# Order of a block's products, masks and stores in the second stage of a two-stage mixer kernel

## The chip, the cores and the metric

The kernel runs on one core of a Trainium2 chip. The metric is the device time of one launch in microseconds (us), the median of several runs. Beside these stands one execution taken with the hardware profiler; all rows below are from that one.

## The reference

One layer `x + RMSNorm_post(Mixer(RMSNorm_pre(x)))` on a prompt of 4096 tokens and on 8 sample streams of 16 tokens, D = 1024. The mixer has a gated linear attention group (4 heads) and an RWKV-7 group (8 heads of 64) that read one input projection and feed one output projection. The change lies in the RWKV-7 group:

```python
def step(s, inp):                      # rwkv7_recurrence, per token
    r_t, w_t, k_t, v_t, kk_t, a_t = inp
    sa = jnp.einsum('bhij,bhj->bhi', s, -kk_t)
    s = (s * w_t[:, :, None, :] + sa[..., None] * (kk_t * a_t)[:, :, None, :]
         + v_t[..., None] * k_t[:, :, None, :])
    y = jnp.einsum('bhij,bhj->bhi', s, r_t)
...
y = ((y - mu) * lax.rsqrt(var + RWKV_GN_EPS)).reshape(B, T, RWKV_WIDTH)   # per head
y = y * rwkv_ln_w + rwkv_ln_b
o_rwkv = (y + bonus) * silu(z_r)
m = jnp.einsum('btc,cd->btd', jnp.concatenate([o_gla, o_rwkv], -1), w_out)
```

## The kernel before

The kernel has two phases. The first (to about 915 us) does the attention group and its projections. The second, `rwkv_phase`, is the one changed. It works on blocks: block 0 holds the 128 sample tokens, blocks 1 to 16 (LAST) hold 256 prompt tokens each. A block has chunks of 64 tokens, four of them for a prompt block. The recurrence is evaluated chunk by chunk in a closed form that needs the inverse of a triangular 64x64 matrix for each chunk and head.

The jobs of one block, and their names in the code:

- `x12, x4, x6, x0, x2, x8, x10`: rounds of the input projection on TensorE, hidden state times weights in split fp16 (three products for each), 128 or 256 output rows each. `x8*4` means four pieces of the round x8; a piece is 8 matmuls of 128x256, and x12 has three pieces, the others six. Each round is then read by ScalarE (`taken`, which writes `praw`) and by VectorE (`mixed`, which writes the operand plane and, as its last instruction, copies the last column to `carry`).
- `lwa0, lwa2` (`rank`, L2140): low-rank products for decay and rate; `kn` and `bs` (`head_sums`, L2179): sums over a head; `clamp`, `rnorm`, `unit`: the key's norm; `k_prime` (L2787, L2788), `beta` (L2801), `a` (`make_a`, L2818), `rkk`, `kappa`, `r`: operands of the recurrence, in `ops`.
- `xs` (`products`, L2158): the block products T^T A of all four chunks, from which the inverse is made. They wait for `beta` and `a` (`op_ok`). `strict:0` and `strict:1` (L2831) mask them into `xb`; `blocks_out` and `blocks_in` on SP's queue store them to DRAM and load them again in another layout; `invert` on GpSimd does 60 dependent steps for the diagonal 32x32 blocks; `inverse_back` stores and reloads the result as `T1` and `TT`, and `td` on VectorE (L2862) transposes `T1`.
- For each chunk: `scores` (L2205), `masked` (VectorE, L2854), `turn` (L2216, L2220), `inner` (L2234), `solve`, `join`, and the state's own chain `meet` (L2289 in the listed rows), `zc` (VectorE, L2886), `unknowns` (L2302), `even`/`odd`, `advance`, `next` (VectorE, L2911, L2913), `keep_y`. `keep_w` (L2870) keeps what `inner` makes; `advance` waits for it.
- For each tile of 128 tokens: `centre`, `variance` (L2357), `deviation`, `normed`, `affine`, `gated`, `high`, `low`: GroupNorm, bonus, gate and the split of m into two fp16 halves; `put_m` stores these.

The order is written out by hand. One table for each engine (`PE_BODY`, `ACT_BODY`, `DVE_BODY`, `SP_BODY`) gives the body for one block b: the projection jobs in it are for block b + 2 (b + 1 with a minus sign), the chunk jobs for block b, and `:4` of `scores`, `inner`, `turn`, `solve`, `join`, `masked`, `keep_w` is the first chunk of block b + 1. `out` marks a point at which work of the output projection is put in near the end of the stage: loads of w_out (`get_ow`), their split into high and low halves (`ow_high` on ScalarE, `ow_low` on VectorE), and jobs that are due when a given number of output units is done. In the last two bodies the pieces of the projection give their place to output units ("room"). Blocks 0 and 1 are prepared by an opening that takes the projection jobs of the same tables in the same order, without chunk jobs.

Four PSUM banks serve all rounds in turn. `ROUND_NO` numbers the rounds in the order of their first piece, bank = number mod 4, and `claim` waits until the round four numbers earlier is read. For x rounds that release is `carry_ok`:

```python
def claim(key):
    m = ROUND_NO[key]
    if m >= NBANK:
        released(ROUND_KEYS[m - NBANK])
    return bank_of(key), m
```

The rounds of a body are numbered in this order: centre:0 (2), x12, bs (2), x4, lw0, la0, lw2, la2, variance:0, x6, x0, kn (2), x2, centre:1 (2), x8, xs0, xs1, variance:1, x10. A counting semaphore `d_full` tells readers that a round is full; its value is the round's number, so rounds must become full in the order of these numbers.

## Time and profile before

| | us |
|---|---|
| median of 3 runs | 2319.01 (2316.41 to 2319.48) |
| profiled execution | 2315.25, its span 2313.5 |
| TensorE busy in the span | 2242.2 (97%) |
| VectorE busy | 1448.1 (63%) |
| ScalarE busy | 1284.4 (56%) |
| GpSimd busy | 578.2 (25%) |
| mean granted clock of TensorE | 0.991 of full speed |

Busy times are sums over a span; times in the rows are us from the span's start. The second phase starts near 925 us; its opening lasts to about 990, the steady bodies to about 1893, block 16's preparation and the last bodies to about 2060, and the rest is the output projection.

### The profile page before, as it was taken

What the parts mean: (1) busy time and instruction counts of PE and PEld (TensorE: products, weight loads), DVE (VectorE), ACT (ScalarE), POOL (GpSimd) and SP (SyncE); (2) the same over time, 40 slices, a digit from 0 to 9 for tenths busy, and PEclk for the clock granted to TensorE, in tenths of its full rate; (3) what the DMA queues carried; (4) which work ended last, traced back from release to release, by engine and by line L of the source; (5) the groups of instructions that cost most, each with busy time, mean ns of one, the idle gap of its engine ahead of it and who ended that gap; (6) DMA issues with size and microseconds to landing.
All of it is one profiled execution on the core that took longest, in us unless ns stands there. A gap on an engine that the chain in (4) does not pass through costs nothing. (4 is left out here: it accounts for less than half of the span.)

```text
span 2313.5 us, 72365 instructions
## 1 busy us (share of the span) xinstructions
PE 2242.2 (97%) x31109; PEld 1704.8 (74%) x31109; DVE 1448.1 (63%) x2699; ACT 1284.4 (56%) x2757; POOL 578.2 (25%) x1070
## 2 busy tenths in 40 slices
PE   7999999999999998889999999999999998899998
PEld 5777777777777776777888888888888886544443
DVE  6444545444455554567777777777777777456675
ACT  8355555555555544645666666666666664343333
POOL 0000000000000000355555555555566565000000
PEclk9999999999999999999999999999999999999999
DMA  6212222222333331222222333232223234666675
GB/s 245 69 56 70 80 79 89 79 79 90 105 108 117 101 101 50 52 59 70 72 72 78 83 87 87 78 81 67 72 82 87 84 88 141 204 213 214 223 237 182
DMA packets 217278, 244.62 MB, mean 106 GB/s; under 512 B 110080, under 2 KB 159552, under 8 KB 212608
## 3 DMA queue, kind: packets, MB, share of 16 engines
q1 hardware_dynamic: 211056, 217.44, 30.8%
q10 hardware_dynamic: 5904, 22.55, 2.7%
q8 instruction: 247, 4.05, 0.7%
q14 instruction: 71, 0.58, 0.1%
HBM read 141.83 MB, written 98.10 MB: 104 GB/s over the span
## 5 line engine op out<-in xcount | busy, mean ns | idle before, releaser
L2111 PE MATMUL first<-h,w_hi 128*128 128x256 f16 (+1 forms) x2496 | 419.1, 272 | 0.0
L2070 POOL TENSOR_TENSOR r_inv_tmp<-r_inv 64x30 f32<-64x30 f32 (+14 forms) x480 | 265.8, 554 | 412.8 <-DMA r_inv<-scratch_blocks 376.5
L748 PE MATMUL d<-h,w_hi 128*128 128x256 f16 (+1 forms) x2176 | 351.6, 270 | 0.0
L2111 PE MATMUL first<-h,w_lo 128*128 128x256 f16 (+1 forms) x1248 | 337.8, 272 | 0.0
L748 PE MATMUL d<-h,w_lo 128*128 128x256 f16 (+1 forms) x1088 | 290.6, 270 | 0.0
L2072 POOL TENSOR_TENSOR r_inv<-r_inv,r_inv_tmp 64x30 f32<-64x30 f32 (+14 forms) x480 | 279.7, 583 | 37.6
L2111 PEld LDWEIGHTS first<-h,w_hi 128*128 128x128 f16 x2496 | 237.6, 98 | 50.4 <-issue 18.9
L748 PEld LDWEIGHTS d<-h,w_hi 128*128 128x128 f16 x2176 | 209.5, 98 | 33.6 <-issue 3.9
L2013 POOL MEMSET r_run_s<- 128x128 f16 x1 | 0.2, 204 | 917.9 <-POOLq L390 917.9
L748 PE MATMUL first<-h,w_hi 128*128 128x256 f16 (+1 forms) x1168 | 184.5, 268 | 5.0 <-DVE w_lo L1236 3.1
L2111 PE MATMUL r_d<-h,w_hi 128*128 128x256 f16 (+1 forms) x960 | 158.8, 271 | 0.8 <-DVE carry_s L2742 0.8
L748 PE MATMUL first<-h,w_lo 128*128 128x256 f16 (+1 forms) x584 | 153.7, 268 | 0.0
L748 PE MATMUL d<-w_hi,h 128*128 128x512 f16 x496 | 147.5, 379 | 0.0
L2111 PEld LDWEIGHTS first<-h,w_lo 128*128 128x128 f16 x1248 | 122.4, 98 | 15.5 <-issue 2.1
L2111 PE MATMUL r_d<-h,w_lo 128*128 128x256 f16 (+1 forms) x480 | 128.9, 271 | 0.0
L748 PEld LDWEIGHTS first<-h,w_hi 128*128 128x128 f16 x1168 | 111.4, 99 | 19.9 <-DVE w_lo L1236 2.9
L748 PEld LDWEIGHTS d<-h,w_lo 128*128 128x128 f16 x1088 | 106.7, 98 | 11.8
L2465 ACT ACTIVATE r_praw<-r_carry 128x2 f32<-128x2 f32 (+1 forms) x112 | 23.0, 205 | 162.6 <-PE first L2111 119.7
L2111 PEld LDWEIGHTS r_d<-h,w_hi 128*128 128x128 f16 x960 | 91.4, 99 | 20.4 <-issue 7.9
L2403 PE MATMUL first<-w_hi,r_ops 128*128 128x512 f16 x352 | 104.7, 379 | 0.0
L1209 DVE SCALAR_TENSOR_TENSOR o_sb<-o_sb,g_norm,o_sq 128x512 f32<-128x512 f32 x33 | 24.8, 751 | 126.0 <-ACT o_sq L1032 126.0
L2738 DVE SCALAR_TENSOR_TENSOR r_ops<-first,sc,r_praw 128x256 f32<-128x256 f32 (+2 forms) x172 | 76.9, 471 | 38.5 <-ACT r_praw L2468 36.4
(393 smaller groups left out, 5129.2 us busy)
## 6 DMA issues: line engine op xcount, KB each, us to landing
h<-in_x SPq DMA_DIRECT2D x33, 512.0 KB, 3.7
r_ops<-in_x SPq DMA_DIRECT2D x33, 512.0 KB, 4.2
out_y<-r_ops SPq DMA_DIRECT2D x33, 512.0 KB, 7.4
scratch_hT<-h SPq DMA_DIRECT2D x16, 1024.0 KB, 7.0
h<-scratch_hT ACTq DMA_DIRECT2D x15, 1024.0 KB, 7.1
scratch_mg<-m_hl SPq DMA_DIRECT2D x33, 256.0 KB, 2.0
r_zr<-scratch_zr SPq DMA_DIRECT2D x33, 256.0 KB, 3.5
r_bon<-scratch_bonus SPq DMA_DIRECT2D x33, 256.0 KB, 5.1
```

Of the source, the lines that this page charges most:

```text
L748: mm = pe.matmul(out, lhs(k, a, w), rhs(k, a, w), start=(n == 0), stop=(n == len(terms) - 1))
L1209: dve.scalar_tensor_tensor(out=o, in0=o, scalar=g_norm[:, 0:1], in1=o_sq[:, :, :], op0=ALU.mult, op1=ALU.mult).then_inc(*m_ok.up(tile))
L2013: pool.memset(m[:, :], v).then_inc(*set_ok.up(0))
L2070: step(pool.tensor_tensor(tmp, inv[0:n, 0:u, u:u + 1].to_broadcast([n, u, w]), inv[0:n, u:u + 1, u + 1:32].to_broadcast([n, u, w]), ALU.mult))
L2072: step(pool.tensor_tensor(inv[0:n, 0:u, u + 1:32], inv[0:n, 0:u, u + 1:32], tmp, ALU.add))
L2111: mm = pe.matmul(out, lhs(k, a, w), rhs(k, a, w), start=(m == 0), stop=(m == 3 * KT - 1))
L2403: mm = pe.matmul(out[:, :], a_part[:, a, k, :], (w_hi_, w_lo_)[w][:, k, :], start=(i == 0 and not more), stop=(i == 11), skip_group_check= ...
L2465: act.activation(praw[:, x % 2, 0:ng, 0], carry[:, g0:g0 + ng], ACT.Copy)
L2738: dve.scalar_tensor_tensor(out=out[to, g], in0=pair[rows, g], scalar=par_s("mu1", g0 + g)[rows], in1=before[rows, g], op0=ALU.mult, op1=AL ...
```

## The change

Jobs change their place in the tables of all four engines; none is added or taken out.

- TensorE: `xs` moves from behind `turn:4` to behind `scores:4`. Four pieces of x8 instead of two now stand before `meet:3`, two instead of four behind it (and behind `xs`). So xs0 and xs1 are full before x8 is, though x8 has the lower claim number.
- For that, `FULL_NO` gives each round a second number in the order in which rounds become full; all waits on `d_full` go by it. Claims and banks still go by `ROUND_NO`.
- VectorE: `clamp:1` before `even:2`; `k_prime` before `next:2`; `low:0` behind `join_o:3`; `beta` and `a` before `td`, `masked:4` and `zc:3`; both `strict` before `mixed:x8`.
- ScalarE: `high:0` behind `rnorm:1`.
- SP: `put_m:0` behind `inverse_back` and two points.

```diff
 PE_BODY
-    x8*2 meet:3 scores:4 out x8*4 inner:4 unknowns:3 turn:4 xs variance:1 out x10*2 advance:3 solve:4 join:4
+    x8*4 meet:3 scores:4 xs out x8*2 inner:4 unknowns:3 turn:4 variance:1 out x10*2 advance:3 solve:4 join:4
 ACT_BODY
-    join_e:2 affine:0 squares:2 out gamma taken:x0 odd:2 turned:3 high:0 rnorm:0 out rnorm:1 z1:3 join_e:3
+    join_e:2 affine:0 squares:2 out gamma taken:x0 odd:2 turned:3 rnorm:0 out rnorm:1 high:0 z1:3 join_e:3
 DVE_BODY
-    clamp:0 even:2 mixed:x0 keep_w:3 clamp:1 low:0 out unit:0 unit:1 next:2 join_o:3 k_prime mixed:x2 out
-    -td masked:4 zc:3 beta a mixed:x8 strict:0 out strict:1 even:3 keep_w:4 normed:1 rkk next:3 join_o:4 gated:1
+    clamp:0 clamp:1 even:2 mixed:x0 keep_w:3 out unit:0 unit:1 k_prime next:2 join_o:3 low:0 mixed:x2 beta out a
+    -td masked:4 zc:3 strict:0 out strict:1 mixed:x8 even:3 keep_w:4 normed:1 rkk next:3 join_o:4 gated:1
 SP_BODY
-    -put_m:1 out -bonus_out out out out get_gate:0 out put_m:0 -inverse_back out out blocks_out blocks_in
+    -put_m:1 out -bonus_out out out out get_gate:0 out -inverse_back out out put_m:0 blocks_out blocks_in
...
+def full_order():
+    ends = {}
+    for n, (job, arg) in enumerate(j for jobs in PE_JOBS for j in jobs):
+        if job == "piece":
+            ends[arg[:2]] = n
+        elif job == "out":
+            ends["out", arg[0], arg[1] // 6] = n
+        elif job in ("xs", "kn", "bs"):
+            ends.update({(arg, job + str(k)): n for k in range(2)})
...
+    return sorted(ROUND_KEYS, key=ends.get)
+FULL_NO = {key: n for n, key in enumerate(full_order())}
...
-                return bank_of(key), m
+                return bank_of(key), FULL_NO[key]
...
-                act.wait_ge(d_full.sem, d_full.at(ROUND_NO[b, r], 1))
+                act.wait_ge(d_full.sem, d_full.at(FULL_NO[b, r], 1))
```

## Rows read from the trace of the kernel before

**Rows 1.** Busy time by stretch: PE, PEld, DVE, ACT, POOL; clock; DMA share; GB/s

```profile
1060.00:1893.00 833.00, 827.25 (x17470) 689.72 (x17461) 628.68 (x1151) 542.26 (x1278) 468.03 (x826) 1.00 0.29 79
1893.00:2075.00 182.00, 166.18 (x2719) 102.36 (x2713) 108.23 (x199) 84.80 (x214) 49.15 (x86) 0.96 0.57 177
```

**Rows 2.** TensorE's waits, 1060 to 1900: us in total, times, longest us

```profile
PE first L2158 <- DVE r_ops L2818: 1.4, 3, 0.6
PE first L2140 <- issue: 1.3, 3, 0.6
```

**Rows 3.** Timeline of TensorE around x8, xs and x10 of one steady period

```profile
1477.57 1.10 PE L2205 MATMUL r_AB<-r_ops 64*64 64x128 f32 x32
...
1482.20 0.43 PE L2234 MATMUL r_EO<-r_TD,h 64*64 64x32 f32 x16
...
1483.42 0.22 PE L2158 MATMUL first<-r_ops 64*64 64x64 f32 x2
...
1484.46 1.12 PE L2357 MATMUL first<-r_y_sq,r_headmean 128*128 128x512 f32 x2
1485.42 0.38 PE L2111 MATMUL first<-h,w_hi 128*128 128x256 f16 x2
...
1487.26 0.69 PE L2311 MATMUL r_EO<-r_bu 128*64 128x64 f32 x16
```

**Rows 4.** Timeline of ScalarE in the same period: taken:x8 and turned:4

```profile
1482.31 0.21 ACT L2465 ACTIVATE r_praw<-r_carry 128x2 f32<-128x2 f32 x1 [5.40 <-PE first L2111]
1482.42 0.83 ACT L2468 ACTIVATE r_praw<-first,sc 128x256 f32<-128x256 f32 x2
...
1483.68 1.09 ACT L2569 ACTIVATE r_bu<-r_AB 128x512 f32<-128x512 f32 x2
```

**Rows 5.** Timeline of VectorE in the same period: next:2, k_prime, a, mixed:x8

```profile
1473.40 0.42 DVE L2911 TENSOR_TENSOR r_S<-r_EO,r_S 128x256 f32<-128x256 f32 x1 [0.92 <-PE r_EO L2272]
...
1474.76 1.23 DVE L2787 TENSOR_TENSOR r_ops<-r_ops,r_scr 128x1024 f32<-128x1024 f32 x1
...
1481.39 1.22 DVE L2818 TENSOR_TENSOR r_ops<-r_ops,r_gam 128x1024 f32<-128x1024 f32 x1
1483.28 1.51 DVE L2738 SCALAR_TENSOR_TENSOR r_ops<-first,sc,r_praw 128x256 f32<-128x256 f32 x3 [0.66 <-ACT r_praw L2468]
1484.82 0.17 DVE L2744 COPY r_carry<-r_praw 128x2 f32<-128x2 f32 x1
```

**Rows 6.** Timeline, all engines, where lwa2 takes the bank of x4

```profile
1509.47 0.16 DVE L2744 COPY r_carry<-r_praw 128x2 f32<-128x2 f32 x1
...
1509.70 0.09 PEld L2140 LDWEIGHTS first<-r_lor,up 64*128 64x128 f16 x1 [0.22 <-issue]
```

**Rows 7.** VectorE's waits, 1060 to 1900

```profile
DVE r_TD L2862 <- DMA r_T<-scratch_inverse: 6.3, 7, 1.5
```

**Rows 8.** TensorE's waits, 900 to 1060 (the opening and the first period)

```profile
PE first L2158 <- DVE r_ops L2818: 4.2, 3, 2.4
```

**Rows 9.** TensorE's waits, 1893 to 2075 (block 16 and the last bodies)

```profile
PE r_EO L2234 <- DVE r_Zc L2886: 9.7, 6, 3.7
...
PE r_d L2158 <- DVE r_ops L2818: 0.9, 1, 0.9
PE r_EO L2311 <- DVE r_Wt L2870: 0.7, 1, 0.7
```

**Rows 10.** Timeline of VectorE at a point of block 16's period

```profile
1922.44 1.28 DVE L2953 SCALAR_TENSOR_TENSOR w_lo<-h,w_hi 128x512 f16<-128x512 f32 x2
```

**Rows 11.** Timeline of ScalarE at the same point

```profile
1920.51 1.15 ACT L2622 ACTIVATE w_hi<-h 128x512 f16<-128x512 f32 x2
```

**Rows 12.** Timeline of SP's queue, block 16's way out

```profile
1977.65 1.24 SPq L1843 DMA_DIRECT2D scratch_mr<-r_m_hl  x1
1978.93 0.49 SPq L1871 DMA_DIRECT2D scratch_inverse<-r_inv  x1
```

**Rows 13.** The store of the inverse, L1871, all 17

```profile
DMA to landing us min/median/max: 1.9/2.9/6.0
```

More of the change, by code:

```diff
@@ L1552 @@
 ROUND_KEYS = list(ROUND_NO)
+def full_order():
[7 more added lines that the diff above has]
+            ends.update({(arg, job + str(k)): n for k in range(2)})
+        elif job == "rank":
+            ends.update({(arg[0], r % arg[1]): n for r in ("lw%d", "la%d")})
+        elif job == "centre":
+            ends.update({(job, arg, k): n for k in range(2)})
+        elif job == "variance":
+            ends[job, arg] = n
+    return sorted(ROUND_KEYS, key=ends.get)
+FULL_NO = {key: n for n, key in enumerate(full_order())}
 AT = {}
@@ L1558 @@
 EARLY = ("x12", "x4", "x6")
-assert [ROUND_NO[0, r] for r in EARLY] == [0, 1, 2]
+assert [ROUND_NO[0, r] for r in EARLY] == [FULL_NO[0, r] for r in EARLY] == [0, 1, 2]
 def rwkv_phase(nc, t, c):
@@ L1893, in get_ow @@
                 if j == 0:
-                    m = ROUND_NO[LAST - 1, "x10"]
+                    m = FULL_NO[LAST - 1, "x10"]
                     sp.wait_ge(d_full.sem, d_full.at(m, 1))
@@ L1901, in get_npost @@
             def get_npost():
-                m = ROUND_NO[LAST, "x10"]
+                m = FULL_NO[LAST, "x10"]
                 sp.wait_ge(d_full.sem, d_full.at(m, 1))
@@ L1911, in fetch @@
                 if tile >= 2:
-                    sp.wait_ge(d_full.sem, d_full.at(ROUND_NO["out", tile - 2, 1], 1))
+                    sp.wait_ge(d_full.sem, d_full.at(FULL_NO["out", tile - 2, 1], 1))
                 sp.dma_start(m_c[:, slot, 0], t["mg"][b][:, i]).then_inc(*mc_in[slot].up(n))
@@ L1923, in get_tw @@
                 if i == 0:
-                    sp.wait_ge(d_full.sem, d_full.at(ROUND_NO[LAST, "x10"], 1))
+                    sp.wait_ge(d_full.sem, d_full.at(FULL_NO[LAST, "x10"], 1))
                     sp.wait_ge(ow_ok.sem, 2 * KT)
@@ L2119, in piece @@
                 n = tiles(b) * P
-                out, m = bank_of((b, r)), ROUND_NO[b, r]
+                out, m = bank_of((b, r)), FULL_NO[b, r]
                 if h == 0 and third == 0:
@@ L2361, in project_out @@
                 h, sixth = n // 6, n % 6
-                m = ROUND_NO["out", tile, h]
+                m = FULL_NO["out", tile, h]
                 out = bank_of(("out", tile, h))
@@ L2435, in load_h @@
                 n = tiles(b) * P
-                act.wait_ge(d_full.sem, d_full.at(ROUND_NO[b - 2, "x10"], 1))
+                act.wait_ge(d_full.sem, d_full.at(FULL_NO[b - 2, "x10"], 1))
                 act.dma_start(hT[:, b % 2, :, :, 0:n], t["hT"][b][:, :, :, 0:n]).then_inc(*h_in[b % 2].up(b // 2 - 1))
@@ L2594, in deviation @@
                 need_ln_set()
-                act.wait_ge(d_full.sem, d_full.at(ROUND_NO["variance", tile], 1))
+                act.wait_ge(d_full.sem, d_full.at(FULL_NO["variance", tile], 1))
                 act.activation(out[:, :], out[:, :], ACT.Ln, bias=const(K_GN)).then_inc(*gr_ok.up(tile))
@@ L2666, in out_squares @@
                 tile, h = arg
-                act.wait_ge(d_full.sem, d_full.at(ROUND_NO["out", tile, h], 1))
+                act.wait_ge(d_full.sem, d_full.at(FULL_NO["out", tile, h], 1))
                 if tile:
@@ L2749, in lor_low @@
                 if b:
-                    dve.wait_ge(d_full.sem, d_full.at(ROUND_NO[b - 1, "la2"], 1))
+                    dve.wait_ge(d_full.sem, d_full.at(FULL_NO[b - 1, "la2"], 1))
                 dve.scalar_tensor_tensor(out=lor[:, 1, 0:n], in0=gin[:, 0, 0:n], scalar=LOR_SCALE, in1=lor[:, 0, 0:n],
```

12 lines of the change are left out of this document (6 added, 6 removed).

## Prediction

> **What bounds the kernel.** I read the busy table by stretch first. In the steady part of the second stage TensorE is busy for 827.25 of 833 us at full granted clock, VectorE for 629 and GpSimd for 468 [rows 1]. So a period of this stage, about 62 us for one block of 256 tokens, is TensorE's program in its written order, and nothing that other engines save is worth anything unless TensorE waits for it. The list of TensorE's waits says how little that is: for the block products (L2158, behind the operand `a`) 1.4 us in three waits over the whole steady part, for the bank of a rank round (L2140) 1.3 us in three [rows 2]. After it, in the last two periods, TensorE loses 9.7 us in six waits for Zc, the longest 3.7 us, and 0.9 and 0.7 us in the period of block 16 [rows 9]. The final stage has no recurrence that this change touches. What can be won is therefore below 10 us. What can be lost is any new wait of TensorE, and a wait inside the period is paid in each period.
>
> The reader then needs TensorE's own order around the edit, with the start of each group [rows 3], and beside it the rows of ScalarE and VectorE that free the bank of x8 [rows 4, 5].
>
> **How a bank comes free.** Four PSUM banks go round. The number that orders them counts rounds by their first piece. x8, xs0, xs1, variance:1, x10 is the order of claims before and after the change, so x10 takes the bank of x8, and its first piece waits for `carry` of x8, the last instruction of mixed:x8. Between the end of x8 and the first piece of x10 TensorE now does inner, unknowns, turn, xs and the variance: 1482.20 to 1485.42, 3.22 us [rows 3]. The release takes in that time: ScalarE starts on x8 at 1482.31, VectorE at 1483.28, and the copy to `carry` ends at 1484.82 + 0.17 = 1484.99 [rows 4, 5]. That is 2.79 us behind the end of x8; the bank is free 0.43 us before it is wanted. Nothing of it shows as a wait, and that is the row on which this prediction rests. That such a claim really holds TensorE is seen one round type earlier: `la2` takes the bank of x4, whose copy ends at 1509.47 + 0.16 = 1509.63, and TensorE's next weight load starts at 1509.70, behind an idle time that the view marks only "issue" [rows 6]. From the copy's end to the matmul I take 0.10 us.
>
> **Part 1: xs ahead of the last two pieces of x8.** No instruction is added. Between scores and the end of x8 there now lie the 64 records of xs (1483.42 to 1484.46, 1.04 us) and 16 matmuls of x8 (1.84 us, as the 16 of x10 from 1485.42 to 1487.26) [rows 3]. The number of changes between fp16 and fp32 groups stays, so I cost them at nothing. But the end of x8 is now nearer to x10 by the length of xs: behind it come only inner, unknowns, turn and variance, 3.22 - 1.04 = 2.18 us, or 2.3 us when turn meets a 128-row product and loses about 0.1 us in the switch. The release still needs 2.79 + 0.10 = 2.89 us behind the end of x8. ScalarE and VectorE can't begin earlier, they wait for x8 itself; the strict masks are over by then. The new wait is 2.89 - 2.29 = 0.6 us. It comes in each period that has a variance between xs and x10, fourteen in all; the one of block 16 is costed apart. Thirteen times 0.6 is **+7.8 us**. Bounds per period: 0.45 us if ScalarE's carry copy (0.21 us) overlaps, 0.8 us if the strict masks or td push mixed:x8 back; so 5.9 to 10.4 us. Behind the waiting x10 stand advance:3, solve and join, so the state's chain moves with it and nothing takes the wait up.
>
> **Part 2: beta and a ahead of td, masked:4, zc:3.** Now `a` ends at 1481.39 + 1.22 = 1482.61, 0.8 us ahead of xs [rows 3, 5]. xs is wanted about 3.2 us earlier. In the new order VectorE comes to beta when mixed:x2 is over, which I step through to about 1477.4, so `a` ends near 1479.7, and TensorE is at xs at 1480.2. About 0.4 us is left; I take no wait, and 0.3 us per period (4 us) as the upper bound. The gain: td waits for the inverse's DMA, 6.3 us in seven waits [rows 7], and `a` behind it is what made TensorE wait at xs. It no longer stands behind td, and strict comes 3 us earlier, so the inverse too. That ends the 1.4 us of [rows 2]: **-1.4 us**; bounds -1.4 and 0.
>
> **Part 3: k_prime ahead of next:2, clamp:1 ahead of even:2, high:0 behind rnorm:1.** k_prime is two instructions of 1.23 us, of which the first is shown [rows 5]. next:2 starts at 1473.40 now and would start near 1474.4. The new state is wanted by meet:3, which now comes two pieces later, over 4 us behind; keep_y on ScalarE follows next:2 and moves by 0.4 us. The cover is those four pieces of x8; without it the price would be 1 us per period. even:2 moves by 0.6 us against 4 us of room. I cost these at nothing.
>
> **Part 4: the opening.** Blocks 0 and 1 have no recurrence as cover. TensorE waits at xs for `a`: 4.2 us in three waits, of which the longest, 2.4, is block 0's and the last, some 1.1, block 2's, in the first period [rows 8]. xs now comes before 16 matmuls of x8 instead of behind them, so the wait grows by them: 0.9 us for block 0 (half as wide) and 1.84 us for block 1, less 0.3 and 0.4 us since rnorm:1 no longer waits for a clamp behind mixed:x0. In block 0 bs0 takes the bank of x8, and mixed:x8 is then late for it, which adds 0.4 us. Together **+2.4 us**, bounds 1 and 3.5. In the first period xs's wait for block 2 goes, and k_prime ahead of next:0 gives about as much back; 0.
>
> **Part 5: block 16's period.** Here two low halves of w_out (1.28 us [rows 10]) stand at each point, and they wait for two high halves on ScalarE (1.15 us [rows 11]). At one point they now stand between beta and `a`: I step xs to wait 2.15 us. At the next they stand between the strict masks, and mixed:x8 now comes behind them. ScalarE's high halves there come behind taken:x8 (0.21 + 0.83, [rows 4]), the odd unknowns and the turned tiles (1.09, [rows 4]): x8's end + 3.8 us. Then a low half, strict:1 and mixed:x8 bring the copy to x8's end + 6.8 us, against 2.3 us of TensorE work: 4.5 us. Now the same period loses 0.9 + 0.7 us [rows 9] and 0.8 us in gaps not listed there. 2.15 + 4.5 - 2.4 = **+4.2 us**, bounds 2 and 6 (a lowered clock behind a stall this long included; the steady part now has none). SP's queue does not move with this stall, and the next loads of w_out land earlier against TensorE: **-1.3 us**, bounds -2 and 0.
>
> **Part 6: put_m:0 behind inverse_back.** In the steady part GpSimd releases inverse_back, so nothing. In block 16's way out SP is the limit: put_m is issued at 1977.65 for 1.24 us, inverse_back at 1978.93 [rows 12]; what it brings back ends the 3.7 us wait of [rows 9]. So 1.28 us come off: **-1.3 us**. That store of the inverse then took the 6.0 us that is the longest landing of its line, median 2.9 [rows 13]. If it lands at the median, 3.1 us more come off; bounds -3.7 (all of the wait) and 0. I keep 6.0, as the loads around it stay. The Trainium skill, "DMA: Bandwidth & Descriptors", where the ~2 us actually goes, puts a transfer's fixed cost at about 2 us and most of that in completion. The row stands at three times that. By the page the whole wait would go and the sum would be 2.4 us less; the trace decides for the row.
>
> **The sum.** 7.8 - 1.4 + 2.4 + 4.2 - 1.3 - 1.3 = +10.4 us. On the profiled execution's 2315.25 us (its span of 2313.5 and 1.75 around it) that is 2325.7. The median of the runs, 2319.01, stands 3.8 us above the profiled one, so I give 2329.4, rounded 2329. Below, 0.2% or 4.6 us is what a measurement of this kernel can tell from no change.
>
> **Rivals.** (A) The forecast, a new wait for x8's bank: 2325 to 2334, chance 0.62. (B) Besides it, `a` comes late by 0.3 us in each period (+4) and the stall of block 16 lowers the clock (+2): about 2335. For it speaks the small room of 0.4 us, against it that my stepping puts nothing else before `a`. 0.18. (C) The bank's wait is half as long, since 0.43 us of room now against 1.04 us taken leaves a price that small changes in issue decide (0.3 us, +4), and the opening and block 16 give back as much as they lose: 2321 to 2323, within 0.2%. 0.15. (D) The other side: the bank's wait is hidden in full, which needs x8 to be released within 2.2 us of its end; then only the earlier inverse counts: -1.4 in the periods, -1.3 in block 2's, and the whole 3.7 us of the tail, with the opening's 2.4 against it and block 16 neutral: -4.0, and with the reloads' 1.3, -5.3: 2314. The point from which it decides is a release under 2.3 us against the 2.79 of [rows 3 to 5], where nothing on VectorE stood in the way in the period shown. 0.05. That the order changes nothing can't be: TensorE's order is the written one.
>
> **Range and chances.** B and C reach to 2335 and 2321. Slower by over 0.2%: A, B and none of C, 0.80. Within: C, 0.15. Faster: D, 0.05. Range 2321 to 2335; A's own is 2325 to 2334.
>
> **What would show it.** In the profile after: idle of about 0.6 us before the first x10 matmul behind L2357, once a period, put down to VectorE's carry (L2744's line) or to issue; the start of x10 0.1 us behind that copy; no wait at L2158 in the steady part but longer ones in the opening; strict about 3 us earlier against the scores; one long stall near block 16; inverse_back ahead of the store of m. TensorE busy time of the steady part unchanged while its length grows by some 6 us. I am wrong if x10 starts right behind the variance there.

## The result: 1.4% slower, and the profile after

The changed kernel takes 2350.48 us (median of 4 runs, 2348.90 to 2353.02) against 2318.42 us for the kernel before; the ratio is 1.014, its 95% interval 1.0123 to 1.0158. The prediction was 2329 us in a range of 2321 to 2335: slower, as forecast, but by 32 us where 10 were forecast, and outside the range. The profiled execution took 2348.90 us, its span is 2347.1 us, 33.6 more than that of before. No instruction was added: the loss is TensorE's idle time and lowered clock.

Busy time by stretch after, in the columns of [rows 1]:

```profile
1060.00:1893.00 833.00, 815.57 (x17029) 675.53 (x17026) 607.02 (x1128) 524.18 (x1245) 460.46 (x802) 1.00 0.29 78
1893.00:2075.00 182.00, 161.08 (x2935) 109.01 (x2935) 104.50 (x192) 83.47 (x205) 69.38 (x114) 0.92 0.46 141
```

TensorE's busy time in the steady stretch fell from 827.25 us to 815.57 [rows 1]: 11.7 us of that stretch are new idle time. The mean clock reads 1.00 in both; after, 3.4 us of the stretch stand at the lower level, 0.50, which is 1.7 us lost. The waits of TensorE in 1060 to 1900, in the columns of [rows 2] (after's lines of this phase have numbers 22 higher than before's, so L2180 is xs, L2133 a piece of a round, L2201 the bs group):

```profile
PE first L2180 <- DVE r_ops L2840: 4.6, 10, 0.5
PE first L2133 <- DVE r_carry L2766: 3.6, 9, 0.4
PE r_d L2201 <- issue: 3.1, 2, 2.5
PE first L2201 <- issue: 1.7, 2, 1.1
PE r_d L2133 <- DVE r_carry L2766: 1.4, 4, 0.4
PE r_d L2180 <- DVE r_ops L2840: 1.4, 3, 0.5
```

(`first` and `r_d` are two tile names for the PSUM banks of rounds; one kind of wait can stand under both.) Three kinds of wait stand where [rows 2] had 1.4 us for the block products: xs for the operand `a` (6.0 us), a piece of x10 for the copy to `carry` (5.0 us), and 4.8 us ahead of matmuls of bs that the view marks only "issue". TensorE around x8, xs and x10 of one period, to be held against [rows 3]:

```profile
1495.06 1.10 PE L2227 MATMUL r_AB<-r_ops 64*64 64x128 f32 x32
1496.62 0.27 PE L2180 MATMUL first<-r_ops 64*64 64x64 f32 x2 [0.46 <-DVE r_ops L2840]
...
1499.57 0.43 PE L2256 MATMUL r_EO<-r_TD,h 64*64 64x32 f32 x16
...
1500.89 1.12 PE L2379 MATMUL first<-r_y_sq,r_headmean 128*128 128x512 f32 x2
1502.41 0.39 PE L2133 MATMUL first<-h,w_hi 128*128 128x256 f16 x2 [0.40 <-DVE r_carry L2766]
```

Scores start at 1495.06, xs only at 1496.62 (1.56 us, 1.56 or 1.57 in all 13 periods; in "store back" below, where xs does not wait, that step takes 0.89 us in each: 0.67 us a period, of which the view lists 0.46 as idle). x8 ends at 1499.57, the variance starts at 1500.89, and x10 at 1502.41; its carry copy ended at 1502.19 + 0.17 = 1502.36, and 0.05 us later TensorE is there. The same stretch of VectorE, then of ScalarE:

```profile
1491.30 0.69 DVE L2970 TENSOR_TENSOR r_m_hl<-r_yT,r_m_hl 128x512 f16<-128x512 f32 x1
1493.27 0.88 DVE L2760 SCALAR_TENSOR_TENSOR r_ops<-first,sc,r_praw 128x256 f32<-128x256 f32 x2 [1.27 <-ACT r_praw L2490]
...
1495.26 1.22 DVE L2840 TENSOR_TENSOR r_ops<-r_ops,r_gam 128x1024 f32<-128x1024 f32 x1
...
1500.64 1.51 DVE L2760 SCALAR_TENSOR_TENSOR r_ops<-first,sc,r_praw 128x256 f32<-128x256 f32 x3 [0.84 <-ACT r_praw L2490]
1502.19 0.17 DVE L2766 COPY r_carry<-r_praw 128x2 f32<-128x2 f32 x1
```

```profile
1492.03 0.38 ACT L2583 ACTIVATE r_yT<-r_EO 128x256 f32<-128x256 f32 x1 [1.79 <-DVE r_m_hl L2970]
1492.31 0.20 ACT L2487 ACTIVATE r_praw<-r_carry 128x2 f32<-128x2 f32 x1
1492.40 0.83 ACT L2490 ACTIVATE r_praw<-first,sc 128x256 f32<-128x256 f32 x2
```

This is the forecast wait of x10: x8's end at 1499.57, mixed:x8 at 1500.64, the copy's end 2.79 us behind x8's end, exactly the release of [rows 3 to 5]. From the variance's start to x10's it takes 1.52 us, against 0.96 in [rows 3]: 0.56 us more, of which the view lists 0.40 as idle. What the prediction did not have is the last fence's first row. ScalarE is idle for 1.79 us ahead of keep_y:2 (L2583, from 1492.03), until VectorE's L2970 ends at 1491.30 + 0.69 = 1491.99; that is low:0, which now stands behind next:2 and join_o:3. Behind keep_y:2 on ScalarE stand taken:x2, then on VectorE mixed:x2 (idle 1.27 us for it), beta and `a`, which ends at 1495.26 + 1.22 = 1496.48: and xs starts at 1496.62.

**Where the 33.6 us went.** Landmarks are the starts of the same group of matmuls (the state's advance of each chunk) in both traces; a difference between landmarks is what a stretch lost.

| stretch | lost, us | of which |
|---|---|---|
| up to the second phase | -1.5 | |
| opening and first period | +6.3 | forecast +2.4 |
| steady periods | +18.9 | x10 13 x 0.56 = 7.3; xs 13 x 0.67 = 8.7 (6.0 listed as idle); inside bs 6.2 against 1.1 before; 1.7 at half clock; the waits of [rows 2] at L2158 gone (1.4 listed) |
| block 16's period | +8.8 | forecast +4.2 - 1.3 |
| last bodies, to the end | +1.1 | forecast -1.3 |

### The profile page after: what moved, and what is told of

Read it like the earlier page. It is cut to its first block and busy times, and to the rows that moved or that the text cites. A ratio compares the mean times of both kernels' runs of the same rounds, so it can differ in the third digit from the quotient of the medians.

```text
span 2347.1 us, 72334 instructions
## 1 busy us (share of the span) xinstructions
PE 2255.8 (96%) x31078; PEld 1713.0 (73%) x31109; DVE 1439.1 (61%) x2699; ACT 1279.3 (55%) x2757; POOL 587.6 (25%) x1070
## 5 line engine op out<-in xcount | busy, mean ns | idle before, releaser
L2133 PE MATMUL first<-h,w_hi 128*128 128x256 f16 (+1 forms) x2496 | 423.9, 275 | 7.8 <-DVE r_carry L2764 4.2
L2092 POOL TENSOR_TENSOR r_inv_tmp<-r_inv 64x30 f32<-64x30 f32 (+14 forms) x480 | 271.7, 566 | 436.4 <-DMA r_inv<-scratch_blocks 400.0
L2133 PE MATMUL first<-h,w_lo 128*128 128x256 f16 (+1 forms) x1248 | 341.4, 275 | 0.0
L2094 POOL TENSOR_TENSOR r_inv<-r_inv,r_inv_tmp 64x30 f32<-64x30 f32 (+14 forms) x480 | 285.1, 594 | 37.6
L2133 PEld LDWEIGHTS first<-h,w_hi 128*128 128x128 f16 x2496 | 239.4, 99 | 60.2 <-issue 13.9
L2133 PE MATMUL r_d<-h,w_hi 128*128 128x256 f16 (+1 forms) x960 | 159.5, 273 | 1.8 <-DVE r_carry L2766 1.4
L2133 PEld LDWEIGHTS first<-h,w_lo 128*128 128x128 f16 x1248 | 123.6, 99 | 17.1 <-issue 2.1
L2133 PE MATMUL r_d<-h,w_lo 128*128 128x256 f16 (+1 forms) x480 | 130.1, 273 | 0.0
L2133 PEld LDWEIGHTS r_d<-h,w_hi 128*128 128x128 f16 x960 | 91.9, 100 | 21.6 <-issue 6.0
L2599 ACT ACTIVATE r_Z<-r_AB 128x256 f32<-128x256 f32 x66 | 25.4, 384 | 140.3 <-PE r_AB L2267 81.0
```

What stands on the lines that cost most here:

```text
L2092: step(pool.tensor_tensor(tmp, inv[0:n, 0:u, u:u + 1].to_broadcast([n, u, w]), inv[0:n, u:u + 1, u + 1:32].to_broadcast([n, u, w]), ALU.mult))
L2094: step(pool.tensor_tensor(inv[0:n, 0:u, u + 1:32], inv[0:n, 0:u, u + 1:32], tmp, ALU.add))
L2133: mm = pe.matmul(out, lhs(k, a, w), rhs(k, a, w), start=(m == 0), stop=(m == 3 * KT - 1))
L2599: act.activation(by_pair(Z1[:, :, :]), pairs(AB, 0), ACT.Copy).then_inc(*z1_ok.up(q))
```

## The experiments

Ratios are to the kernel before, each with runs of both on one chip; one point of 0.001 is 2.3 us, and most intervals are 0.001 to 0.002 to either side. The kernel before itself had medians of 2318.0 to 2322.2 us on these chips, so runs of different groups are compared by their ratios, and differences of medians between them can be off by some 4 us.

| run | median us | ratio | 95% interval |
|---|---|---|---|
| the change | 2350.5 | 1.014 | 1.0123 to 1.0158 |
| store back | 2335.8 | 1.0062 | 1.0042 to 1.0082 |
| xs back | 2374.6 | 1.023 | 1.0206 to 1.0253 |
| both back | 2366.6 | 1.0188 | 1.0164 to 1.0212 |
| five pieces ahead | 2338.9 | 1.0076 | 1.0055 to 1.0097 |
| store late, on before | 2325.8 | 1.002 | 1.0009 to 1.0031 |
| variance behind x10 | 2374.9 | 1.023 | 1.0216 to 1.0244 |
| opening of before | 2350.0 | 1.0118 | 1.0103 to 1.0134 |
| points behind | 2345.1 | 1.0103 | 1.0087 to 1.0119 |
| load later | 2343.4 | 1.0109 | 1.0091 to 1.0127 |
| three mended | 2326.2 | 1.0032 | 1.0018 to 1.0045 |
| rotation | 2353.8 | 1.0154 | 1.0138 to 1.0171 |
| before with two edits | 2320.4 | 1.0005 | 0.9995 to 1.0014 |
| three mended, opening of the change | 2333.1 | 1.0053 | 1.0035 to 1.007 |
| three mended, load later | 2320.2 | 0.9986 | 0.9976 to 0.9996 |
| three mended, put_m late | 2331.6 | 1.0041 | 1.0026 to 1.0057 |

**Store back.** The edit to the changed kernel:

```diff
-    join_e:2 affine:0 squares:2 out gamma taken:x0 odd:2 turned:3 rnorm:0 out rnorm:1 high:0 z1:3 join_e:3
+    join_e:2 affine:0 squares:2 out gamma taken:x0 odd:2 turned:3 high:0 rnorm:0 out rnorm:1 z1:3 join_e:3
-    clamp:0 clamp:1 even:2 mixed:x0 keep_w:3 out unit:0 unit:1 k_prime next:2 join_o:3 low:0 mixed:x2 beta out a
+    clamp:0 clamp:1 even:2 mixed:x0 keep_w:3 low:0 out unit:0 unit:1 k_prime next:2 join_o:3 mixed:x2 beta out a
-    -put_m:1 out -bonus_out out out out get_gate:0 out -inverse_back out out put_m:0 blocks_out blocks_in
+    -put_m:1 out -bonus_out out out out get_gate:0 out put_m:0 -inverse_back out out blocks_out blocks_in
```

> The changed kernel with high:0, low:0 and put_m:0 back at the points that they had before. Theory: the wait of xs for the operand a, 0.5 us in each period, comes from keep_y:2 on ScalarE, which writes the tile that low:0 reads and now waits until low:0 has come behind join_o:3; with low:0 early again that wait goes (6.0 us over the steady part), the wait of x10 for the bank of x8 stays at 0.56 us a period: 2344 us. Rival: a is late by itself, since xs is wanted 3.2 us earlier and VectorE has the same work ahead of it; then the wait stays and the time is that of the change, 2350 us.

Measured: 2335.8 us, ratio 1.0062. The trace has no wait at L2180 in the steady part, and x10's waits stay (3.4 + 1.4 us). keep_y:2 now waits for the state alone, on ScalarE:

```profile
1488.24 0.38 ACT L2583 ACTIVATE r_yT<-r_EO 128x256 f32<-128x256 f32 x1 [0.94 <-DVE r_S L2933]
1488.52 0.20 ACT L2487 ACTIVATE r_praw<-r_carry 128x2 f32<-128x2 f32 x1
```

So the theory of xs's wait holds, and the rival (`a` late by itself) falls. The gain is 15 us by the medians, 18 by the ratios, where 6 were expected. The expectation took the listed 6.0 us for xs's price. By the step from scores to xs it is 8.7 us; besides, the trace lost 2.4 us less in block 16's period, 2.5 us less at a chunk of the tail (below, put_m) and had no half clock in the steady part (1.7 us). Together that is 15.3 us. Three steps were put back at once; that low:0 and not high:0 holds up keep_y:2 is read from the trace of the change, where L2970 starts at 1491.30 right behind other work of VectorE.

**xs back, both back.** TensorE's line as before, first with everything else of the change, then with the store's edits as well:

```diff
-    x8*4 meet:3 scores:4 xs out x8*2 inner:4 unknowns:3 turn:4 variance:1 out x10*2 advance:3 solve:4 join:4
+    x8*2 meet:3 scores:4 out x8*4 inner:4 unknowns:3 turn:4 xs variance:1 out x10*2 advance:3 solve:4 join:4
```

> The changed kernel with TensorE's line alone as before: two pieces of x8 ahead of meet:3, four behind scores:4, xs behind turn:4. Theory: both waits of the steady part go (x10's 0.56 us x 13 and xs's 6.0 us), with them most of the opening's loss and of the stall of block 16, since a and the bank both get their room back: 2350.5 - 7.3 - 6.0 - 4 - 4 = 2329 us; what is left over the kernel before is then the stalls at bs. Rival: the other half of the change, on VectorE and ScalarE, costs by itself more than 10 us, and the time stays above 2335 us.

> Both edits of the two runs before it: what is left of the change is VectorE's order alone (clamp:1 and k_prime early, beta, a and the strict masks ahead of td's and mixed:x8's places). Theory: low:0's place costs something only where xs stands early, so this is as the run with xs back, within 2 us, about 2328 us; if the stalls at bs belong to TensorE's order they go too and it is 2320 us, the time of the kernel before. Rival: low:0's place costs the same in either order, and this is 6 us faster than the run with xs back.

Both theories missed, and both rivals held: VectorE's and ScalarE's half costs over 10 us by itself (54 us by the medians), and with the store back too it is 8 us faster. Measured: 2374.6 us, ratio 1.023, and 2366.6 us, ratio 1.0188. TensorE's waits of "xs back":

```profile
PE first L2133 <- DVE r_carry L2766: 17.4, 9, 1.9
PE r_EO L2256 <- DVE r_Zc L2908: 9.4, 13, 0.7
PE r_d L2133 <- DVE r_carry L2766: 5.8, 3, 1.9
```

In the change VectorE's strict masks stand ahead of mixed:x8. Strict masks need xs; with xs behind turn:4 again, x8's bank is released only behind xs and both masks, and x10 waits 1.9 us in each period. Besides, the clock stood at its lower level three times in the steady part of "xs back" and five times in that of "both back", for 3.4 us each, which costs 5 and 8.5 us. The two tables are a pair: VectorE's half of the change without TensorE's is worse than both together (1.023 and 1.0188 against 1.014); TensorE's half alone was not run. The pair of runs also says that low:0's late place costs here too, through Zc (9.4 us in 13 waits, none with the store back), so the theory that it costs only where xs stands early was too narrow.

**Five pieces of x8 ahead of meet:3, one behind xs.**

```diff
-    x8*4 meet:3 scores:4 xs out x8*2 inner:4 unknowns:3 turn:4 variance:1 out x10*2 advance:3 solve:4 join:4
+    x8*5 meet:3 scores:4 xs out x8 inner:4 unknowns:3 turn:4 variance:1 out x10*2 advance:3 solve:4 join:4
```

> The changed kernel with five pieces of x8 ahead of meet:3 and one behind xs, for four and two: x8 ends 0.92 us earlier against x10, and xs comes 0.92 us later. Theory: x10's wait of 0.56 us and xs's of 0.5 us both go, less room for nothing else: 2350.5 - 7.3 - 6.0 = 2337 us, and 2 us less where block 16's stall and the opening shrink with them. Rival: the waits are not of the bank's and of a's room but of the switch between the fp16 and fp32 groups, which stays: 2350 us. A second rival: meet:3 comes 0.92 us later and the state's chain moves what it frees, new waits at zc or next, over 2350 us.

Measured: 2338.9 us, ratio 1.0076. xs's wait is gone, x10's is not (3.3 us in 9 waits). The expectation had a slip in it: the number of x8's pieces behind xs does not change what lies between x8's end and x10 (inner, unknowns, turn, variance), so the bank has no more room. From x8's end to the first piece of x10 it takes 2.85 us in this run and in the change. That the time came within 2 us of the forecast is luck, since 7.3 us of its sum did not come. The first rival falls with xs's wait. The second falls too: no new wait at zc or next. What is new is an idle time of 2.2 us inside turn (L2238) that the view marks only "issue".

**The store alone, on the kernel before.**

```diff
-    join_e:2 affine:0 squares:2 out gamma taken:x0 odd:2 turned:3 high:0 rnorm:0 out rnorm:1 z1:3 join_e:3
+    join_e:2 affine:0 squares:2 out gamma taken:x0 odd:2 turned:3 rnorm:0 out rnorm:1 high:0 z1:3 join_e:3
-    clamp:0 even:2 mixed:x0 keep_w:3 clamp:1 low:0 out unit:0 unit:1 next:2 join_o:3 k_prime mixed:x2 out
+    clamp:0 even:2 mixed:x0 keep_w:3 clamp:1 out unit:0 unit:1 next:2 join_o:3 low:0 k_prime mixed:x2 out
-    -put_m:1 out -bonus_out out out out get_gate:0 out put_m:0 -inverse_back out out blocks_out blocks_in
+    -put_m:1 out -bonus_out out out out get_gate:0 out -inverse_back out out put_m:0 blocks_out blocks_in
```

> The kernel before with one part of the change alone: high:0 behind rnorm:1, low:0 behind join_o:3, put_m:0 behind the inverse's way out. The wait of keep_y:2 for low:0 then delays taken:x2 and with it a, but here a has 0.8 us of room at xs. Theory (low:0's place costs only where xs stands early): 2319 to 2322 us, no wait at xs. Rival (it costs in either order): a wait at xs of 0.5 us a period, 2325 us.

Measured: 2325.8 us, ratio 1.002: the time of the rival, and not by its mechanism. The steady part of the trace loses nothing against before (0.0 us by the landmarks), with one wait of 0.6 us at xs where before had three: `a` has its 0.8 us of room there, as the theory says. Most of the trace's loss lies in the tail (6.5 us at one chunk), where the profile shows put_m:0 late:

```profile
2009.44 0.63 ACT L2614 ACTIVATE r_m_hl<-r_yT 128x512 f16<-128x512 f32 x1 [5.93 <-DMA scratch_mr<-r_m_hl]
```

high:1 waits 5.93 us for the store of m to land, and TensorE then stands 5.1 us for VectorE's mask of the scores behind it.

**variance:1 behind two pieces of x10.** To "store back":

```diff
-    x8*4 meet:3 scores:4 xs out x8*2 inner:4 unknowns:3 turn:4 variance:1 out x10*2 advance:3 solve:4 join:4
+    x8*4 meet:3 scores:4 xs out x8*2 inner:4 unknowns:3 turn:4 out x10*2 variance:1 advance:3 solve:4 join:4
```

> The run with the store back (2335.8 us), and with variance:1 behind the first two pieces of x10 in place of ahead of them. x10 then takes the bank that centre:1 had, free long before, and variance:1 takes x8's bank 1.85 us later than x10 wanted it. Theory (x10's wait is that for x8's bank): the 0.56 us a period go, 2328 us. Rival (the 0.56 us are the variance's own latency, or VectorE is late and the wait moves to variance:1 or to next): no gain, 2335 us.

Measured: 2374.9 us, ratio 1.023, 39 us more than "store back". Neither theory's time, but the trace decides between them. TensorE's timeline:

```profile
1515.17 0.41 PE L2242 MATMUL r_AB<-r_ident,r_ops 64*64 64x64 f32 x16
1515.52 0.39 PE L2133 MATMUL first<-h,w_hi 128*128 128x256 f16 x2
...
1528.97 0.39 PE L2133 MATMUL first<-h,w_hi 128*128 128x256 f16 x2 [3.28 <-DVE r_carry L2766]
```

x10 (1515.52) starts 0.35 us behind the start of turn's last group (1515.17), with no wait: x10's 0.56 us was the bank of x8, and the variance that comes later takes that bank without a wait. The new wait is of the same kind. The four banks are handed round in the order of claims; moving one claim moved every pairing behind it, and x12 of the next body now takes the bank of x10: 3.28 us in each period, behind x10's carry copy.

**The opening in the order of before.** The opening's three lists are made from the tables of before, the bodies from those of the change.

> The changed kernel, with the opening (blocks 0 and 1) in the order of the tables before. Theory (the 6.2 us lost up to the second period are xs ahead of x8's last pieces, k_prime and the strict masks in the opening): about 5 us less than the change, 2345 us. Rival (they are lost in the first period, to VectorE's order there, or to a lowered clock that comes in both): 2349 to 2351 us.

> The run with three things mended (2326.2 us), with the opening in the order of the change again. In the traces taken so far the stretch up to the first period was 6.1 to 8.7 us longer than before with the opening of the change, 1.9 to 3.1 with that of before. Theory (the opening costs its own 3 to 4 us): 2329.5 us. Rival (it is execution noise of the granted clock, as the equal medians of the change with either opening say): 2326 us.

Measured: 2350.0 us and ratio 1.0118 against 1.014 for the first; 2333.1 us and 1.0053 against 1.0032 for the second. Both differences of ratios are some 5 us for the opening's order, but in each pair the intervals overlap, and the medians of the first pair differ by 0.5 us only: neither pair alone is clear of the noise. In the traces of the second pair the stretch up to the first period differs by 7.3 us; TensorE waits 4.9 us for `a` at xs against 3.1, and the granted clock over 926 to 1060 is 0.90 against 0.95. The two were not separated. "Store back" has the opening and the first period in the same order as the change, and there its trace loses 8.7 us where that of the change loses 6.3. After's waits in 900 to 1060, to be held against [rows 8]:

```profile
PE first L2180 <- DVE r_ops L2840: 4.9, 2, 2.9
...
PE r_EO L2333 <- DVE r_ops L2941: 1.4, 1, 1.4
```

The second row is new: k_prime ahead of next:0 in the first period, which the prediction cancelled against a gain.

**Points behind `a` and behind mixed:x8.**

```diff
-    clamp:0 clamp:1 even:2 mixed:x0 keep_w:3 out unit:0 unit:1 k_prime next:2 join_o:3 low:0 mixed:x2 beta out a
-    -td masked:4 zc:3 strict:0 out strict:1 mixed:x8 even:3 keep_w:4 normed:1 rkk next:3 join_o:4 gated:1
+    clamp:0 clamp:1 even:2 mixed:x0 keep_w:3 out unit:0 unit:1 k_prime next:2 join_o:3 low:0 mixed:x2 beta a out
+    -td masked:4 zc:3 strict:0 strict:1 mixed:x8 out even:3 keep_w:4 normed:1 rkk next:3 join_o:4 gated:1
```

> The changed kernel, with the point between beta and a moved behind a, and the point between the strict masks moved behind mixed:x8 on VectorE; only block 16's period and the two after it have work at these points. Theory: the low halves of w_out there (1.28 us each point) are what makes xs wait 2.4 us and x10 4.4 us in block 16's period, and the half clock behind it follows from that stall: 6 to 8 us less, 2343 to 2345 us. Rival: ScalarE's high halves and its tiles come first, and the wait stays at 3 us or more: 2348 us.

Measured: 2345.1 us, ratio 1.0103, 5 us less by the medians and 9 by the ratios, as the theory says. In the change, block 16's period had these two waits on TensorE, and on VectorE the rows that make them:

```profile
PE first L2133 <- DVE r_carry L2764: 4.2, 1, 4.2
PE r_d L2180 <- DVE r_ops L2840: 2.9, 1, 2.9
```

```profile
1940.04 1.28 DVE L2975 SCALAR_TENSOR_TENSOR w_lo<-h,w_hi 128x512 f16<-128x512 f32 x2
1941.25 1.22 DVE L2840 TENSOR_TENSOR r_ops<-r_ops,r_gam 128x1024 f32<-128x1024 f32 x1
...
1950.23 1.29 DVE L2975 SCALAR_TENSOR_TENSOR w_lo<-h,w_hi 128x512 f16<-128x512 f32 x2 [5.00 <-ACT w_hi L2644]
1951.44 0.68 DVE L2853 TENSOR_TENSOR r_xb<-first,r_mask_p 128x512 f32<-128x512 f32 x1
...
1953.58 0.16 DVE L2764 TENSOR_SCALAR r_carry<-first 128x2 f32<-128x2 f32 x1
```

One low half of w_out between beta and `a` (1.28 us), the next between the strict masks: it waits 5.00 us for ScalarE's high half, and mixed:x8 and the copy stand behind it. Behind that stall TensorE ran at 0.50 of its clock, the lower of its two levels:

```profile
1953.80:1957.20 3.40, 3.40 (x16) 2.23 (x16) 2.28 (x4) 1.65 (x4) 0.00 (x0) 0.50 0.53 94
```

With the points moved, the first chunk behind these waits comes 0.9 us late against the end of the steady part, in place of 9.3, and TensorE's longest waits in 1893 to 2075 that concern it are

```profile
PE r_EO L2311 <- ACT r_yT L2583: 3.3, 1, 3.3
PE r_d L2180 <- DVE r_ops L2840: 1.7, 1, 1.7
...
PE first L2133 <- DVE r_carry L2764: 0.3, 1, 0.3
```

some of which comes back one chunk later (3.3 us), so 4 us net in the trace. That ScalarE's own work comes first (the rival) is wrong.

**The load of the next activations behind keep_y:0.**

```diff
-    -taken:x10 -load_h centred:0 taken:x12 odd:0 turned:1 tanh_w out z1:1 join_e:1 keep_y:0 taken:x4 tanh:lw0
+    -taken:x10 centred:0 taken:x12 odd:0 turned:1 tanh_w out z1:1 join_e:1 keep_y:0 -load_h taken:x4 tanh:lw0
```

> The changed kernel with the load of the next activations (1 MB, issued by ScalarE right behind taken:x10) behind keep_y:0. In the trace of the changed kernel each of the four stalls inside bs ends 1.3 to 1.5 us behind the landing of a 16 KB packet of the instruction queue, while that load fills the DMA engines. Theory (TensorE stands there for its instructions, and that load makes them late): the four stalls (6.2 us) and the half clock behind the first (1.7 us) go or shrink, 2343 to 2345 us. Rival (they are late whatever else is loaded): the stalls stay, 2350 us.

What it tests. In the change TensorE stood still four times inside bs, in every third period, in the middle of a group where no semaphore is waited for. The longest of them, on TensorE, and the busy times around it:

```profile
1132.81 0.38 PE L2201 MATMUL first<-r_scr,r_rk_sum 64*64 64x256 f32 x2
1135.72 0.43 PE L2201 MATMUL r_d<-r_scr,r_rk_sum 64*64 64x256 f32 x2 [2.53 <-issue]
```

```profile
1132.00:1136.00 4.00, 1.47 (x67) 0.94 (x59) 1.16 (x4) 3.52 (x7) 3.45 (x8) 1.00 0.35 126
1136.00:1139.40 3.40, 3.40 (x27) 2.39 (x20) 2.42 (x3) 0.09 (x1) 3.17 (x4) 0.68 0.02 5
```

Between 1132.81 and 1135.72 it started nothing (2.53 us idle), and over 1136.0 to 1139.4 its granted clock was 0.68 in the mean: the lower level began at 1137.2 and held for 3.4 us. The DMA view of 1133.3 to 1134.3 shows one packet of the instruction queue:

```profile
q1 hardware_dynamic: 51, 0.08, 21.1%
...
q8 instruction: 1, 0.02, 5.5%
```

From the packet records (us, those of 16 KB):

```
kernel    packet starts + takes    TensorE goes on   behind the landing
after     1133.34 + 0.88           1135.72           1.51
after     1325.21 + 0.88           1327.52           1.43
after     1514.77 + 0.99           1517.17           1.41
after     1704.86 + 0.96           1707.09           1.27
before    1125.32 + 1.07           1127.85           1.46
```

Measured with the load moved: 2343.4 us, ratio 1.0109, and no stall inside bs at all; the steady part of the trace loses 9.6 us (landmarks of chunks 5 and 53) where the change lost 17.7. So TensorE stood there for its instructions, and the 1 MB load, which ScalarE issues at 1510.06 and which takes 6.7 us at the median to land, is what made them late (it is issued 5.8 to 6.2 us ahead of the point where TensorE stops, in all four cases). The theory holds, in place and in size.

The traces of all runs say more than these five cases. Twelve of the kernels have such stalls inside bs, 42 in all, from 0.6 to 2.9 us; in each one TensorE goes on 1.25 to 1.57 us behind the landing of a 16 KB instruction packet. Such packets come every 5.7 us at the median of the trace of before, but the one that ends a stall comes 7.6 to 10.9 us behind the one ahead of it. The other thing that it could wait for, the landing of the load itself, is out: TensorE goes on between 1.3 us ahead of it and 1.9 us behind it. The three kernels with the load moved have no stall there. "Variance behind x10" has none either, with the load in its old place; there TensorE waits 3.28 us ahead of bs, in each period, for something else; and in "rotation" bs waits for a bank in every period, so that a stall there could not be told apart.

**Three mended.** Store back, points behind, opening of before, all at once.

> The changed kernel with three things mended at once: high:0, low:0 and put_m:0 at their points of before, the points of block 16 behind a and behind mixed:x8, and the opening in the order of before. What is left is xs ahead of x8's last pieces, with x10's wait for x8's bank. Theory (the parts add): 2335.8 - 5.3 (points) - 1.5 (opening) = 2329 us, x10's wait unchanged at 0.56 us a period. Rival (they overlap, since the stalls and the lowered clock move): 2333 us or more.

Measured: 2326.2 us, ratio 1.0032. The theory gave 2329 us: the parts add up to within the intervals. What remains of the change is xs ahead of x8's last pieces and what goes with it, with x10's wait (3.5 + 1.2 us in the list of waits).

**Rotation.** To "three mended":

```diff
-    meet:0 scores:1 centre:0 x12*3 inner:1 unknowns:0 turn:1 -bs x4*2 out x4 advance:0 solve:1 join:1 x4*3 lwa0
+    meet:0 scores:1 x12*3 centre:0 inner:1 unknowns:0 turn:1 -bs x4*2 out x4 advance:0 solve:1 join:1 x4*3 lwa0
-    x8*4 meet:3 scores:4 xs out x8*2 inner:4 unknowns:3 turn:4 variance:1 out x10*2 advance:3 solve:4 join:4
+    x8*4 meet:3 scores:4 xs out x8*2 inner:4 unknowns:3 turn:4 out x10*2 variance:1 advance:3 solve:4 join:4
-    -taken:x10 -load_h centred:0 taken:x12 odd:0 turned:1 tanh_w out z1:1 join_e:1 keep_y:0 taken:x4 tanh:lw0
+    -taken:x10 -load_h taken:x12 centred:0 odd:0 turned:1 tanh_w out z1:1 join_e:1 keep_y:0 taken:x4 tanh:lw0
```

> The run with three things mended, and the order of claims changed so that nobody takes x8's or x10's bank early: variance:1 behind two pieces of x10, centre:0 behind the pieces of x12 (on ScalarE too). x10 then takes the bank of centre:1, variance:1 that of x8 1.85 us later than x10 did, centre:0 those of xs1 and x10 behind x12's 2.7 us; bs1 takes that of x12 and may wait 0.3 us. Theory (only the bank numbers make the wait): no wait at x10 and none at centre, 2329 - 7.3 + 3.9 = 2326 us or somewhat less. Rival (the wait goes to the next taker): waits of over 0.5 us a period at centre or bs, 2329 us or more.

```profile
PE first L2225 <- issue: 13.6, 9, 1.5
PE first L2395 <- issue: 8.1, 9, 1.1
```

Measured: 2353.8 us, ratio 1.0154. The rival holds. x10 waits for nothing, and the two takers that the expectation named, bs (L2225, for the bank of x12) and centre (L2395, for that of x10), now wait 1.5 and 1.1 us in each period, where 0.3 and nothing were expected: 29 us listed with the `r_d` halves, for 5 listed before. (Lines of the runs with the opening of before stand another 24 higher.)

**The kernel before with two edits.**

```diff
-    -taken:x10 -load_h centred:0 taken:x12 odd:0 turned:1 tanh_w out z1:1 join_e:1 keep_y:0 taken:x4 tanh:lw0
+    -taken:x10 centred:0 taken:x12 odd:0 turned:1 tanh_w out z1:1 join_e:1 keep_y:0 -load_h taken:x4 tanh:lw0
-    clamp:0 even:2 mixed:x0 keep_w:3 clamp:1 low:0 out unit:0 unit:1 next:2 join_o:3 k_prime mixed:x2 out
-    -td masked:4 zc:3 beta a mixed:x8 strict:0 out strict:1 even:3 keep_w:4 normed:1 rkk next:3 join_o:4 gated:1
+    clamp:0 even:2 mixed:x0 keep_w:3 clamp:1 low:0 out unit:0 unit:1 next:2 join_o:3 k_prime mixed:x2 beta out a
+    -td masked:4 zc:3 mixed:x8 strict:0 out strict:1 even:3 keep_w:4 normed:1 rkk next:3 join_o:4 gated:1
```

> The kernel before with what the other runs point to as harmless or useful: beta and a ahead of td, mixed:x8 still ahead of the strict masks, and the load of the next activations behind keep_y:0. TensorE's order stays that of before. Theory: the waits at the block products (1.4 us) and the stalls inside bs (1.1 us) go, 2 us less than before: within 0.2%, on its lower side. Rival: a ahead of td makes td and with it the inverse late, a wait for Zc in the periods, slower by 0.2% or more.

Measured: 2320.4 us, ratio 1.0005, no difference. The stalls inside bs are gone (1.1 us in the profile of before), the waits at the block products too, and in their place Zc waits 5.2 us in 13 waits of up to 0.8 us. The rival's mechanism is there, and its price is about what the other two gave.

**What is left of x10's wait; put_m:0 alone.** "Three mended" with the load of the activations later, and "three mended" with put_m:0 late again:

> The run with three things mended, with the load of the next activations behind keep_y:0 too. Theory (what is left over the kernel before is x10's wait and 2 to 3 us of stalls inside bs over those of before): the stalls go, 2323 us. Rival: 2326 us, the stalls come back at another instruction.

> The run with three things mended, with put_m:0 alone behind the inverse's way out again. Theory: in the last bodies the store of m then stands on SP behind the loads of the output units, high:1 waits for its landing, and the chain of the last chunks with it; 2 to 6 us, 2328 to 2332 us, with the wait of ScalarE for that store back in the trace. Rival (the forecast of part 6): the store of the inverse is issued 1.3 us earlier and the tail is that much shorter, 2325 us.

Measured: 2320.2 us, ratio 0.9986 (0.9976 to 0.9996), and 2331.6 us, ratio 1.0041. The first has x10's wait in full (3.6 + 1.2 us listed) and no stall inside bs, and is the fastest version of the study, though by less than the 0.2% that the prediction set as its bound. It gained 11 us on "three mended" by the ratios, 6 by the medians, where the profiled execution of that run shows 3.9 us of stalls; that other executions have more of them is likely and was not shown. The second costs about 2 us by the ratios (its interval overlaps that of "three mended", so this is not clear of the noise) and 5 by the medians, with ScalarE's wait for the store of m back in the trace (6.0 us in two waits).

## Why the prediction was wrong in size

The sum forecast +10.4 us and the trace lost 33.6. Part 1 came as forecast; the step that failed is in part 3.

**Part 1, the bank of x8: right, in mechanism and size.** 0.56 us a period against 0.6, the release 2.79 us against 2.79, seen as a wait on the carry copy. Shown by "variance behind x10", where the wait at x10 went with the bank. Rival (D) is out.

**Part 2, beta and `a` ahead of td: right on its own.** With low:0 in its old place `a` is in time and L2158's 1.4 us are gone. But the sentence "I take no wait" failed in the change, because of part 3.

**Part 3 is the step that failed.** "keep_y on ScalarE follows next:2 and moves by 0.4 us" looked at one producer of keep_y's operands. keep_y:2 also overwrites the tile that low:0 reads, and low:0 was moved behind join_o:3 by the same diff. The part listed k_prime, clamp:1 and high:0, and not low:0. The step was costed at nothing. Its price: xs comes 0.67 us late in each steady period, 8.7 us in all, and 2.4 us in block 16's period; putting the three store steps back gave 15 us. Rival (B) had the right symptom (`a` late by 0.3 us a period) with no cause, and half its size.

**The stalls for instructions were in no part.** The trace of before had one (1.1 us), in the same view as [rows 2] as

```profile
PE r_d L2179 <- issue: 0.7, 1, 0.7
```

and the prediction did not read it. In the change they were 6.2 us plus 1.7 us at the lower clock. Moving one load took them away ("load later", 7 us). Why they are longer with the change than in the one profile of before is not settled: "store late, on before" has 3.3 us of them with TensorE's order untouched, so part of the difference is from execution to execution.

**Part 4, the opening: mis-sized.** +2.4 forecast; the two pairs of runs give some 5 us, neither clear of the noise, and the trace 6.3. The waits themselves grew by less than forecast: at xs they are 4.9 us against 4.2. The 0 for the first period was wrong: k_prime ahead of next:0 costs 1.4 us. Most of the rest is a lowered clock (0.93 over 926 to 1060 after, 0.96 before; by these means an estimate of 4 us over 134), which the part did not cost, and which differs between executions with the same opening (0.90 in "store back").

**Part 5, block 16: mechanism right, the clock left out of the sum.** xs waits 2.9 us (2.15 forecast), x10 4.2 us listed (4.5 forecast for the whole). The same chunks before, then after:

```profile
1861.60:1926.20 64.60, 62.15 (x1303) 51.47 (x1301) 51.51 (x95) 44.41 (x104) 36.33 (x61) 1.00 0.39 106
1885.30:1959.20 73.90, 66.14 (x1304) 53.93 (x1300) 51.19 (x95) 44.70 (x105) 36.04 (x61) 0.93 0.35 97
```

TensorE's idle time grew from 2.45 to 7.76 us, by 5.3 where 4.2 were forecast. Its busy time grew by 4.0 us with the same work, at a mean clock of 0.93 for 1.00: that part is the lowered clock, which the prediction had in its bounds and not in its sum. Of the 1.3 us that it took off for earlier loads of w_out nothing is seen; no run isolates them. "Points behind" takes most of the loss away.

**Part 6, put_m:0: wrong sign.** The forecast looked at the queue where put_m:0 used to stand, and not at who waits for its landing. In the last bodies the store of m now stands on SP behind the loads of the output units, and ScalarE's high:1 waits for it. SP's queue and ScalarE's wait after:

```profile
2026.27 0.68 SPq L1955 DMA_DIRECT2D r_scr<-scratch_tw  x1
2026.99 0.71 SPq L1865 DMA_DIRECT2D scratch_mr<-r_m_hl  x1
2033.29 0.53 SPq L1859 DMA_DIRECT2D r_zr<-scratch_zr  x1
```

```profile
ACT r_m_hl L2636 <- DMA scratch_mr<-r_m_hl: 5.7, 2, 3.4
```

Before, the same tile's store was issued at 1977.65 [rows 12], 6 us behind its high half (1971.78), and there is no such wait; after, it is issued 22 us behind its high half (2004.78). It costs 2.5 us at one chunk here; in the one run that moves it alone 2 us by the ratios, not clear of the noise. The store of the inverse did come 1.3 us earlier against the load ahead of it, and it landed in 6.6 us (6.0 before), so to keep the row's 6.0 us was right; the longest wait for Zc is 3.2 us against 3.7.

## What to carry to other kernels

For every moved instruction list its readers and its writers over the whole ring of buffers: the one that overwrites what it reads (here keep_y, behind low:0) waits as surely as the one that reads what it writes. Banks handed round by order of claims pair steps that have nothing to do with each other, so moving one claim re-pairs all behind it; write down each taker and the release it waits for, before and after. A queue position is worth what the last waiter on the landing loses, not what the next transfer in the queue gains.

## What was not expected of the hardware

TensorE stood still for 0.6 to 2.9 us in the middle of a group without any semaphore, and went on 1.25 to 1.57 us behind the landing of a 16 KB packet of the instruction queue, in 42 of 42 cases in twelve traces; a 1 MB load that ScalarE issued some 6 us earlier brought it on, and moving that load away ended it, in three kernels. bs stands behind 80 short fp32 matmuls that pass in 1.2 us (inner, unknowns and turn, 1514.38 to 1515.59); whether that matters was not tested.

The granted clock fell behind some idle times and not behind others of the same length, so what a stall costs can't be read from its own length. In the change it fell to its lower level for 3.4 us behind the 2.53 us of idle time inside bs, for 6.8 us around the 4.2 us at x10, and also behind the 1.4 us that k_prime costs ahead of next:0; it did not fall behind the other three stalls of bs. In "both back" x10 waits 1.95 us in each of 13 periods, and the clock fell behind five of them; in "opening of before" two idle times of 2.2 us passed at full clock.
